# Two-layer hybrid decoder on one core: fp32 queries and embedding gate, twelve query and key weight pieces in borrowed buffers, the next layer's weights held back

## The reference

```
q = (h @ w_q).reshape(B, S, 8 heads, 2, 128)
s1 = q[..., 0, :] . sub_k1 ;  s2 = q[..., 1, :] . sub_k2        # 128 keys each
top 16 of each, top 16 of their sums  ->  16 expert rows per token and head
act = gelu(u_tab[row] . h);  peer = sum(act * softmax weight * v_tab[row])
ple = sigmoid(h @ ple_gate) * (p @ ple_proj)
h = layer_norm(ALPHA * h + peer + ple)
```

## Time and profile before

| | us |
|---|---|
| median of 3 runs | 2046.44 |
| lowest, highest | 2045.86, 2052.09 |
| profiled execution | 2055.09 |
| its span | 2053.2 |
| PE busy | 1767.3 (86%) |
| DVE busy | 1421.4 (69%) |
| ACT busy | 952.1 (46%) |
| POOL busy | 733.9 (36%) |
| block 0's rows, layer 0: from its first dot product to block 1's first | 348.01 to 710.89 |
| the same in layer 1 | 1377.76 to 1729.74 |

### The profile page before, as it was taken

How to read it: one execution, slowest core, us unless ns; L and a number is a source line. 1 busy time by engine, 2 the same in 40 slices (tenths; PEclk the granted TensorE clock), 3 DMA queues, 4 the chain that set the end, 5 groups by cost and what they waited for, 6 DMA issues and landing times. The chain is left out here.

```text
span 2053.2 us, 26948 instructions
## 1 busy us (share of the span) xinstructions
PE 1767.3 (86%) x7560; PEld 1045.6 (51%) x7560; DVE 1421.4 (69%) x3512; ACT 952.1 (46%) x2277; POOL 733.9 (36%) x595
## 2 busy tenths in 40 slices
PE   8989999798889787788799899997888898778876
PEld 7977877344445322222279778773444453222222
DVE  5765566887777777776558645667877788777764
ACT  5545442444455544444345454424444564444443
POOL 0110002454444456565400100024444445556553
PEclk9999999999999999999999989999999999999999
DMA  6523456999999999999845324569999999999997
GB/s 238 167 91 103 137 151 228 408 405 425 425 426 426 418 425 426 427 426 427 346 135 163 93 94 133 154 221 412 399 426 426 426 409 426 426 426 426 426 426 300
DMA packets 108028, 660.62 MB, mean 322 GB/s; under 512 B 12032, under 2 KB 14224, under 8 KB 41360
## 3 DMA queue, kind: packets, MB, share of 16 engines
q0 software_dynamic: 75376, 546.57, 63.9%
q1 hardware_dynamic: 32544, 112.71, 16.8%
HBM read 658.17 MB, written 1.06 MB: 321 GB/s over the span
## 5 line engine op out<-in xcount | busy, mean ns | idle before, releaser
L716 PE MATMUL acc<-arena 128*128 128x512 f32 x896 | 443.5, 623 | 119.9 <-ACT arena L1116 119.1
L697 PE MATMUL acc<-arena 128*128 128x512 f32 x896 | 420.0, 611 | 68.8 <-ACT arena L1090 68.2
L571 POOL DMA_INDIRECT arena<-experts_dram,idxu x224 | 273.4, 1221 | 283.6 <-PE acc L697 251.5
L592 POOL DMA_INDIRECT arena<-experts_dram,stage x224 | 295.1, 1317 | 218.4 <-PE acc L716 157.8
L1474 DVE CUSTOM_DVE_ANT_0 arena<-arena,h 128x1024 f32<-128x1024 f32 x224 | 274.6, 1226 | 139.9 <-DMA arena<-experts_dram,stage 74.2
L716 PEld LDWEIGHTS acc<-arena 128*128 128x128 f32 x896 | 158.2, 193 | 404.2 <-issue 403.7
L1444 DVE CUSTOM_DVE_ANT_0 arena<-arena,h 128x1024 f32<-128x1024 f32 x224 | 274.3, 1225 | 94.5 <-DMA arena<-experts_dram,idxu 91.2
L1356 DVE TENSOR_TENSOR raw_r<-raw,w_hi 128x1024 fp32r<-128x1024 f32 x184 | 219.6, 1222 | 142.2 <-ACT w_hi L1014 140.4
L697 PEld LDWEIGHTS acc<-arena 128*128 128x128 f32 x896 | 165.4, 193 | 299.6 <-issue 160.8
L1014 ACT ACTIVATE w_hi<-raw 128x1024 fp32r<-128x1024 f32 x188 | 191.5, 1051 | 79.1 <-DMA raw<-weights_dram 57.3
L1110 ACT ACTIVATE gel<-dots 128x1 f32<-128x1 f32 x256 | 51.9, 203 | 292.1 <-DVE dots L1474 291.6
(11 more groups left out here) (290 smaller groups left out, 2732.3 us busy)
## 6 DMA issues: line engine op xcount, KB each, us to landing
raw<-weights_dram SPq DMA_DIRECT2D x204, 512.0 KB, 3.7
lnr<-lnrows_dram POOLq DMA_DIRECT2D x4, 1024.0 KB, 5.2
arena<-experts_dram,idxu POOLq DMA_INDIRECT x224, 13.2
arena<-experts_dram,stage POOLq DMA_INDIRECT x224, 14.0
lnr<-cum_dram POOLq DMA_DIRECT2D x2, 1024.0 KB, 8.6
raw<-weights_dram SPq DMA_DIRECT2D x16, 128.0 KB, 6.9
cst<-consts_dram SPq DMA_DIRECT2D x1, 1448.0 KB, 12.6
par<-params_dram POOLq DMA_DIRECT2D x2, 616.0 KB, 10.5
```

The costliest lines, as they stand in the source:

```text
L571: nc.gpsimd.indirect_dma_start(slots[n % RING][:, :], None, experts[:, :], bass.IndirectOffsetOnAxis(idxu[:, n:n + 1], 0)).then_inc(slot_i ...
L592: nc.gpsimd.indirect_dma_start(slots[i % RING][:, :], None, experts[:, :], bass.IndirectOffsetOnAxis(stage[:, i:i + 1], 0)).then_inc(slot_ ...
L697: last = mm(acc[:, c * 512:(c + 1) * 512], diag[:, i % 4, :], slots[n % RING][:, D + c * 512:D + (c + 1) * 512], start=False, stop=n == RA ...
L716: last = mm(acc[:, c * 512:(c + 1) * 512], diag[:, i % 4, :], slots[i % RING][:, D + c * 512:D + (c + 1) * 512], start=False, stop=ends)
```

## The change

- **Queries and embedding gate in fp32.** Heads 3 to 7 take the fp32 path of heads 1 and 2. The gate's pieces go through the new `embedding_piece`, one fp32 product in place of three fp32r ones. With that go 18 weight pieces' splits a layer on ACT, DVE and POOL, and the split of h (`h1hi`). `h1w` moves from slot 7 to the first half of `hidden`, and row 7's two waits go.
- **Twelve pieces in free buffers.** The ten query pieces of heads 3 to 7 and two full key pieces (the keys of heads 1 to 7, packed, with the same bytes in all) leave the ring of seven (`EXTRAS`): six go to the `w_hi` buffers, two to `emb_gate`, two to `base`, two to the second half of `hidden`. SP issues them in its own order: four after the last transpose "mT" has been made and ahead of the last piece of "out"; two when `w_hi` buffers come free in "out"; six after the last "out" product.
- **Next layer held back.** SP waits, ahead of the next layer's first piece, until all but four rows of the layer are used (`last_rows`). POOL issues `par` behind the same wait. ACT and DVE split the first group at ("ln2", 1) and at "smallT".
- The steps "pp" and "pgw" move by some rows: the gate's pieces stand every fourth row from (5, 5) to (7, 1), where they stood every third from (5, 7) to (6, 13).

```diff
-    s += [("h1T", 0, 0), ("h1T", 0, 1), ("h1hi", 0), ("stats", 1), ("ln1", 1), ("wq0", 0), ("sc", 0, 0)]
-    s += [("h1T", 1, 0), ("h1T", 1, 1), ("select", 0), ("h1hi", 1), ("wq0", 1), ("sc", 1, 0), ("texp", 0)]
+    s += [("h1T", 0, 0), ("h1T", 0, 1), ("stats", 1), ("ln1", 1), ("wq0", 0), ("sc", 0, 0)]
+    s += [("h1T", 1, 0), ("h1T", 1, 1), ("select", 0), ("wq0", 1), ("sc", 1, 0), ("texp", 0)]
     s += [("wqh", 0, 1), ("wq", 0, 1), ("sc", 0, 1), ("sc", 1, 1)]
     s += [("wqh", 1, 0), ("wq", 1, 0), ("sc", 0, 2), ("sc", 1, 2)]
     beside = {(0, 9): [("wqh", 1, 1)], (0, 12): [("wq", 1, 1)], (0, 14): [("sc", 0, 3), ("sc", 1, 3)]}
     beside |= {(hd - 3, 3): [("wqh", hd // 2, hd % 2)] for hd in range(4, EH)}
     beside |= {(hd - 3, 6): [("wq", hd // 2, hd % 2)] for hd in range(4, EH)}
     beside |= {(hd - 3, 9): [("sc", 0, hd), ("sc", 1, hd)] for hd in range(4, EH)}
-    beside |= {(5, 1): [("pp", 0, 0), ("pp", 1, 0)], (5, 4): [("pp", 0, 1), ("pp", 1, 1)]}
-    beside |= {at: [("pgw", 0, j)] for j, at in enumerate(((5, 7), (5, 10), (5, 13), (6, 0)))}
-    beside |= {at: [("pgw", 1, j)] for j, at in enumerate(((6, 4), (6, 7), (6, 10), (6, 13)))}
-    beside |= {(6 + c, 2 - c): [("pg", c, 0), ("pg", c, 1)] for c in range(2)}
+    beside |= {(4, 12): [("pp", 0, 0), ("pp", 1, 0)], (5, 2): [("pp", 0, 1), ("pp", 1, 1)]}
+    beside |= {at: [("pgw", 0, j)] for j, at in enumerate(((5, 5), (5, 9), (5, 13), (6, 1)))}
+    beside |= {at: [("pgw", 1, j)] for j, at in enumerate(((6, 5), (6, 9), (6, 13), (7, 1)))}
+    beside |= {(6 + c, 2): [("pg", c, 0), ("pg", c, 1)] for c in range(2)}
...
-            g.append(([made], hd >= RAW_HEADS, [None, made]))
+            g.append(([made], False, [None if hd < RING_HEADS else made, made]))
         else:
             g.append(([("wq0", 0), ("wq0", 1)], False, [("wq0", 1), ("wq0", 1)]))
-        g.append(([("sc", 0, hd), ("sc", 1, hd)], False, [("sc", 1, hd)]))
+            g.append(([("sc", 0, 0), ("sc", 1, 0)], False, [("sc", 1, 0)]))
+            g.append(([("sc", b, hd) for hd in range(1, EH) for b in range(NB)], False, [("sc", 1, 4), ("sc", 1, EH - 1)]))
     g.append(([("pp", c, b) for b in range(2) for c in range(2)], False, [("pp", 0, 1), ("pp", 1, 1)]))
     for c in range(2):
-        g.append(([("pg", c, 0), ("pg", c, 1)], True, [None, None, None, ("pg", c, 1)]))
+        g.append(([("pg", c, 0), ("pg", c, 1)], False, [None, None, None, ("pg", c, 1)]))
...
+EXTRAS = [(GROUP_OF["wq", hd // 2, hd % 2], j) for hd in range(RING_HEADS, EH) for j in range(2)]
+EXTRAS += [(GROUP_OF["sc", 0, 1], j) for j in range(2)]
+RING_PIECES = [piece for piece in PIECES if piece not in EXTRAS]
...
+        h1w = hidden[:, 0:KT * T].rearrange("p (k t) -> p k t", k=KT)
...
+        def extra_home(L, piece):
+            e = EXTRAS.index(piece)
+            if e < HIS:
+                return hi_all[:, hi_slot(L, e) * PIECE:][:, 0:PIECE]
+            if e < HIS + 2:
+                return emb_gate[:, e - HIS, :]
+            if e < HIS + 4:
+                return base[:, e - HIS - 2, :]
+            return hidden[:, KT * T + (e - HIS - 4) * PIECE:][:, 0:PIECE]
+        def extra_free(L, piece):
+            e = EXTRAS.index(piece)
+            if e < HIS:
+                return used(L, SPLIT_PIECES[e - HIS])
+            return filled(L, ("mT", 1, 1) if e < HIS + 4 else ("out", 1, 1))
...
+        def last_rows(L):
+            return row_used, RING + (L + 1) * NB * RANKS - 4
...
-            stream = [(L, piece) for L in range(DEPTH) for piece in PIECES]
-            for n, (L, piece) in enumerate(stream):
+            o = RING_PIECES.index((GROUP_OF["out", 1, 0], 3))
+            ahead = {o: EXTRAS[HIS:HIS + 4], o + 3: EXTRAS[0:1], o + 4: EXTRAS[1:2], RING_PIECES.index((GROUP_OF["pp", 0, 0], 0)): EXTRAS[HIS + 4:] + EXTRAS[2:HIS]}
+            stream = [(L, i, piece) for L in range(DEPTH) for i, piece in enumerate(RING_PIECES)]
+            for n, (L, i, piece) in enumerate(stream):
+                if L and i == 0:
+                    sp.wait_ge(*last_rows(L - 1))
+                for extra in ahead.get(i, ()):
+                    sp.wait_ge(*extra_free(L, extra))
+                    cols = 3 * 2 * P if extra == EXTRAS[-1] else PIECE
+                    sp.dma_start(extra_home(L, extra)[:, 0:cols], weights[L * len(PIECES) + PIECES.index(extra)][:, 0:cols]).then_inc(extra_in[EXTRAS.index(extra)], 16)
                 if n >= RAWS:
-                    sp.wait_ge(*used(*stream[n - RAWS]))
+                    old, _, last = stream[n - RAWS]
+                    sp.wait_ge(*used(old, last))
...
-                    if kind == "h1hi":
-                        b = step[1]
-                        tok = slice(b * P, (b + 1) * P)
-                        for q in range(2):
-                            ks = slice(4 * q, 4 * q + 4)
-                            pool.wait_ge(h1_hi_ready, 2 * (L * NB + b) + q + 1)
-                            nc.gpsimd.tensor_tensor(hT[:, 1, ks, tok], h1w[:, ks, tok], hT[:, 0, ks, tok].bitcast(F32), ALU.subtract).then_inc(h1_lo_ready, 1)
-                    for piece in LO_SPLIT_AT.get(step, ()):
-                        if piece in POOL_LO:
-                            n, rs = split_number(L, piece), raw_slot(L, piece)
-                            pool.wait_ge(w_hi_ready, n + 1)
-                            nc.gpsimd.tensor_tensor(w_lo[:, rs, :], raw[:, rs, :], w_hi[:, n % HIS, :].bitcast(F32), ALU.subtract).then_inc(pool_lo_ready, 1)
...
-                        if n == RING - 1:
-                            pool.wait_ge(*filled(L, ("wq", 1, 0)))
-                            pool.wait_ge(h1_lo_ready, 4 * (L + 1))
...
-                        if n == RANKS - 1 and L + 1 < DEPTH:
-                            pool.wait_ge(*filled(L, ("pp", 1, 1)))
-                            pool.dma_start(par[:, :], params[L + 1]).then_inc(params_in, 16)
                     if kind == "experts":
                         b = step[1]
                         n0 = (L * NB + b) * RANKS
@@ -593,6 +586,9 @@
                                     slots[i % RING][:, :], None, experts[:, :],
                                     bass.IndirectOffsetOnAxis(stage[:, i:i + 1], 0)).then_inc(slot_in[i % RING], 16)
                     if kind == "ln2" and step[1] == 1 and L + 1 < DEPTH:
+                        pool.wait_ge(*filled(L, ("pp", 1, 1)))
+                        pool.wait_ge(*last_rows(L))
+                        pool.dma_start(par[:, :], params[L + 1]).then_inc(params_in, 16)
...
-                if GROUPS[g][1]:
-                    pe.wait_ge(h1_lo_ready, 4 * (L + 1))
-                    return feature_half(L, g, ps, i, i)
...
+            def embedding_piece(L, g, j, blocks):
+                w = whole(L, g, j)
+                for ps, b in blocks:
+                    for i in range(2):
+                        k = 2 * j + i
+                        ends[b] = mm(ps, h1w[:, k, b * P:(b + 1) * P], w[:, i * 512:(i + 1) * 512], start=k == 0, stop=k == KT - 1)
...
-                    if L == 0 and step == ("smallT",):
-                        for piece in first_group(0):
+                    if step == ("smallT",):
+                        for piece in first_group(L)[2 if L else 0:]:
                             split_hi(*piece)
-                    if step == ("ln2", 0):
-                        for piece in first_group(L + 1):
+                    if step == ("ln2", 1):
+                        for piece in first_group(L + 1)[0:2]:
...
+                    if step == ("smallT",):
+                        for piece in first_group(L)[1 if L else 0:]:
+                            split_lo(*piece)
+                    if step == ("ln2", 1):
+                        for piece in first_group(L + 1)[0:1]:
                             split_lo(*piece)
...
-                                if beside == "split" and i % 3 == 2 and i // 3 < len(first_group(L + 1)):
-                                    split_lo(*first_group(L + 1)[i // 3])
```

More of the change, by code:

```diff
@@ L147, in steps @@
     return s
-NO_BANK = {"wide", "wide_out", "late", "softplus", "onorm", "stats", "ln1", "ln2", "select", "texp", "h1hi", "wqh", "pgw", "row", "experts"}
+NO_BANK = {"wide", "wide_out", "late", "softplus", "onorm", "stats", "ln1", "ln2", "select", "texp", "wqh", "pgw", "row", "experts"}
 STEPS = steps()
@@ L193 @@
 SPLIT_PIECES = [(i, j) for i, j in PIECES if GROUPS[i][1]]
-COUNTED = [(i, j) for i, j in PIECES if GROUPS[i][2][j] is None]
+EXTRAS = [(GROUP_OF["wq", hd // 2, hd % 2], j) for hd in range(RING_HEADS, EH) for j in range(2)]
+EXTRAS += [(GROUP_OF["sc", 0, 1], j) for j in range(2)]
+RING_PIECES = [piece for piece in PIECES if piece not in EXTRAS]
+COUNTED = [(i, j) for i, j in RING_PIECES if GROUPS[i][2][j] is None]
 def dense_splits(lo):
-    order = [i for i, g in enumerate(GROUPS) if g[1] and g[0][0][0] not in ("wq", "pg")]
+    order = [i for i, g in enumerate(GROUPS) if g[1]]
     at = {}
@@ L206, in dense_splits @@
```

(33 more changed lines are left out.)

49 lines of the change are left out of this document (17 added, 32 removed).

## The result

| | before | after |
|---|---|---|
| median of 6 runs | 2049.76 | 2028.8 |
| lowest, highest | 2045.86, 2052.09 | 2026.36, 2030.88 |
| ratio, 95% interval | | 0.9904 [0.9888, 0.992] |
| profiled execution, its span | 2055.09, 2053.2 | 2027.38, 2025.4 |
| mixed part, layer 0 and 1 | 362.9, 352.0 | 351.2, 349.3 |

The change made the kernel some 20 us faster. 2005 was forecast, with 1988 to 2022 as the range: the direction was right, the size half of what I said, and the time lies outside the range.

What follows compares the result with a forecast made beforehand. DMA engines were taken to bound the long stage of rows, other engines the dense stage. 26.9 + 16.0 + 1.8 - 3 = 41.7 off the profiled 2055.09, or 2004.7 from the median 2046.44, rounded to 2005; range 1988 to 2022.

Steps and rivals of the forecast that it cites:

- mixed part: From block 0's first dot product to block 1's: forecast 336 us in both layers, from 362.9 and 352.0.
- PE may cost 5.8 ... take 342 as the upper bound: Heads 4 to 6 of the rows: PE needs 127.6 us against 121.8 of bytes, so mixed part at most 342.
- The left-over: Mixed part's time beyond its bytes, 11.6 and 10.8 us, where the ring of rows runs short; kept at 11.
- Rival 1: PE paces heads 4 to 6 of the rows: mixed part 342, time 2017; chance 0.16.
- Bytes that leave: Query, key and next-layer pieces and par leave the mixed part: 26.9 us gained in layer 0, 16.0 in layer 1.
- the 10.9 between the layers: Old difference between the layers' mixed parts, against 10.1 us of next-layer pieces and par; forecast to go.
- rival 2: The moved pieces don't land before the rows; 12 pieces stay in each mixed part: 2034; chance 0.05.
- The first row: Start of the mixed part: without POOL's subtraction of h the first row comes 0.9 earlier, 1.8 us for two layers.
- The added wait: At the layer boundary, SP's wait for layer 0's 252nd row costs 3 us, bounds 0 and 10.
- Rival 4: PE, not the DMA engines, paces the whole mixed part; added fp32 work makes it slower, 2073; chance 0.06.

Runs made afterwards that it cites:

- e1: The changed kernel with the step pg four rows later on ACT and DVE; median 2012.5, ratio to before 0.9826.
- e11: The changed kernel with ACT's and DVE's copies of queries and key scores two rows later, pp three, pg left in place; 2006.01, ratio to before 0.9776.
- e4: The changed kernel with ACT's and DVE's steps behind queries and key scores two rows later, behind pp and gate three; 2000.17, ratio to before 0.9765.
- e6: The kernel before with ACT's and DVE's steps for queries and key scores two rows later, pp and pg three; 2046.23, ratio to before 0.9985.
- e9: e4 with half of the embedding gate's products left out; 2000.77, ratio to before 0.9765.
- e2: The changed kernel with only one of every two products of the embedding gate; 2014.08, ratio to before 0.9827.
- e7: e4 without SP's wait for the last rows ahead of the next layer's first piece; 2005.55, ratio to before 0.9798.

## Why the prediction was wrong

- **The step that failed** is "PE may cost 5.8 ... take 342 as the upper bound" of the mixed part, with the moved steps themselves costed at nothing. I counted bytes and PE's own work, and bounded from above by the larger sum. The row of the diff that moves pg from two and four rows behind the product to one I had read and not priced. I took a step's place in PE's order for its place in time. The added gate work puts PE some four rows behind DVE there, so a step one row behind a product waits for these rows and the product. The mixed part measured 351.2 and 349.3 instead of 336. e1 shows 8.7 and 6.7 of that to be pg's, e11 shows 11.2 and 10.6 for the other copies alone (the two overlap), and e4 (334.1 and 332.8) that 17.1 and 16.5 are waits in order. Those other copies stood as near to their products before; there too I had priced only PE's 1.5 behind each, not the stand of ACT and DVE.
- **The left-over.** I carried the old 11 over as a constant. It was 26.3 and 24.4 after, and 9.2 and 7.9 in e4. Two things made it so. The waits grew: DVE's at pg from 4.9 to 15.5 in layer 0 and at tsum from 9.3 to 17.7. And before, some of the waits were hidden behind bytes (e6: the late copies win 3 there, 28.6 after); when the bytes went, the waits came out. How much is due to each, no run shows. Rival 1, PE pacing heads 4 to 6, named nearly the right place. But PE's work there is as summed, 128.1 in e4 (row 64 to row 112) against 127.6, and costs nothing by itself (e9); what it did was to lengthen the waits (e2). Rival 1 gave 2017, which is also too fast.
- **Bytes that leave** were right: heads 1 to 4 take 39.0 to 40.9 against 39.4 of bytes, the 10.9 between the layers gone (351.2 against 349.3), the twelve pieces issued from 300 to 328 and in ahead of the first dot, rival 2 out. With the waits taken away the sum of both mixed parts shrinks by 45.9 against 42.9 forecast.
- **The first row** was not. The index comes 0.9 earlier, as forecast, but the row takes 1.9 longer to be there. Counted from the first h1T, the first dot is 1.0 later in layer 0 and 0.2 in layer 1 (24.3 to 24.5), so the term was -1.2 instead of +1.8. That the dot at 347.10 stands 0.9 before the old one is chance: other kernels with the same start have it from 343.8 to 350.0.
- **The added wait** cost 0.8 instead of 3, and in e7 against e4 the dense stage behind it doesn't differ (348.9, 348.8). On the guess that a piece's packets are smaller than a row's, the trace agrees: 4096 bytes against 8192. Rival 4, PE pacing everything, is out by the result, which is faster, and by e9.

In numbers: 41.7 forecast; the measured medians differ by 21.0 and the rows of the profiled runs by 19.3. The in-order waits at the copies of PE's results are worth 28.6 (e4 against after), more than the missing 20.7: with them gone the rows have shrunk by 48.9 against before, 7 more than the 41.7 forecast for the whole; 2 of these 7 are from waits that before had too (rows of e6).
